# A modulation vector's work moved from a dense layer into the mixer before it, and that layer in two phases by seven products

## The reference, cut to what matters

```python
def rms_norm(x, g): ...
for layer in range(2):
    mod = silu(c) @ ada_w[layer] + ada_b[layer]        # 1024 -> 6 * 1024
    shift_m, scale_m, gate_m, shift_f, scale_f, gate_f = split(mod, 6)
    h = rms_norm(x, norm_mix_g[layer]) * (1 + scale_m) + shift_m
    x = x + gate_m * (hybrid mixer(h) if layer == 0 else conv module(h))
    h = rms_norm(x, norm_ffn_g[layer]) * (1 + scale_f) + shift_f
    x = x + gate_f * ((silu(h @ w_gate[layer]) * (h @ w_up[layer])) @ w_down[layer])
return rms_norm(x, final_norm_g)                       # x: 256 rows of 1024
```

## Time and profile before

| | us |
|---|---|
| median of the runs | 1461.85 (1460.13 to 1463.21) |
| the profiled execution | 1465.13 |
| its span, first to last instruction | 1463.4 |

### The profile page before, as it was taken

How to read it: one execution, slowest core, us unless ns; L and a number is a source line. 1 busy time by engine, 2 the same in 40 slices (tenths; PEclk the granted TensorE clock), 3 DMA queues, 4 the chain that set the end, 5 groups by cost and what they waited for, 6 DMA issues and landing times. The chain is left out here.

```text
span 1463.4 us, 18944 instructions
## 1 busy us (share of the span) xinstructions
PE 1376.3 (94%) x7517; PEld 1015.5 (69%) x7517; DVE 870.7 (60%) x1464; ACT 275.6 (19%) x602; POOL 265.6 (18%) x342
## 2 busy tenths in 40 slices
PE   5999999896776999999999999999999999999997
PEld 1877655653442788768888888777766878888843
DVE  2458775432232668753454685788783874777864
ACT  2222221000000311643345101000002113211101
POOL 5078010000000300553355402100020100000000
PEclk9999999998888999999999999999999999999999
DMA  9976887899999697866774455898854552555431
GB/s 350 310 263 226 285 329 298 348 417 415 416 418 385 191 305 261 306 194 162 159 180 133 160 162 176 327 333 322 297 210 150 155 156 73 163 168 172 170 129 47
DMA packets 176057, 355.58 MB, mean 243 GB/s; under 512 B 7289, under 2 KB 137041, under 8 KB 158561
## 3 DMA queue, kind: packets, MB, share of 16 engines
q1 hardware_dynamic: 166720, 313.64, 60.4%
q0 software_dynamic: 9248, 40.71, 9.5%
HBM read 352.58 MB, written 1.74 MB: 242 GB/s over the span
## 5 line engine op out<-in xcount | busy, mean ns | idle before, releaser
L1846 PE MATMUL PS<-HT,ring 128*128 128x256 f32 x1152 | 258.3, 382 | 0.1
L1846 PEld LDWEIGHTS PS<-HT,ring 128*128 128x128 f32 x1152 | 215.5, 190 | 36.0 <-issue 7.9
L1542 DVE TENSOR_TENSOR X<-X,PS 128x1024 f32<-128x1024 f32 x14 | 17.1, 1222 | 113.2 <-PE PS L1318 113.2
L1265 PE MATMUL PS<-ring_extra,slot_rows 128*32 128x256 f32 x576 | 56.3, 450 | 27.6 <-DMA ring_extra<-in_expert_w_gate 7.1
L2876 PE MATMUL PS<-HT,ring 128*128 128x256 f32 x352 | 76.8, 379 | 0.0
L2905 PE MATMUL PS<-ada_stage,half_sums 128*128 128x256 f32 x320 | 75.6, 379 | 0.0
L2905 PE MATMUL PS<-ring,half_sums 128*128 128x256 f32 x320 | 75.6, 379 | 0.0
L2876 PEld LDWEIGHTS PS<-HT,ring 128*128 128x128 f32 x352 | 66.7, 190 | 9.0
L2882 PE MATMUL PS<-ring,hid 128*128 128x512 f32 x160 | 71.8, 592 | 0.0
L2905 PE MATMUL PS<-ring,HT 128*128 128x256 f32 x304 | 68.8, 379 | 0.0
L2905 PEld LDWEIGHTS PS<-ring,half_sums 128*128 128x128 f32 x320 | 59.4, 190 | 11.2 <-issue 4.3
(11 more groups left out here) (736 smaller groups left out, 2465.4 us busy)
## 6 DMA issues: line engine op xcount, KB each, us to landing
ring<-in_hy_w_in SPq DMA_DIRECT2D x40, 1024.0 KB, 8.4
ring_extra<-in_w_ada SPq DMA_DIRECT2D x24, 1024.0 KB, 7.9
ada_stage<-in_ada_w POOLq DMA_DIRECT2D x24, 1024.0 KB, 7.3
ring<-in_ffn_w_gate SPq DMA_DIRECT2D x22, 1024.0 KB, 5.9
ring<-in_ffn_w_up SPq DMA_DIRECT2D x22, 1024.0 KB, 5.8
ring<-in_ffn_w_down SPq DMA_DIRECT2D x22, 1024.0 KB, 5.8
ring_extra<-in_expert_w_down SPq DMA_DIRECT2D x18, 1024.0 KB, 22.9
ring_extra<-in_expert_w_up SPq DMA_DIRECT2D x18, 1024.0 KB, 20.1
```

The lines of the kernel that those rows point to most:

```text
L1265: mm = pe.matmul(PS[e * SLOTS:(e + 1) * SLOTS, 2, j * CW:(j + 1) * CW], hs[:, k, e * SLOTS:(e + 1) * SLOTS], w[e][:, k, :], start=(k == 0) ...
L1542: dve.tensor_tensor(part, part, PS[:, 6:8, :], ALU.add).then_inc(added, 1)
L1846: mm = pe.matmul(dst, w[:, k, half * P:(half + 1) * P], HT[:, k, :], start=(k == 0), stop=(k == KT - 1))
```

## The change

- The third modulation's loads, adds, sums and transposes leave the first dense layer. In the mixer SP loads the 24 pieces in turns into two buffers (the memory of `BC`, and `stage`), DVE adds each at a position of `THIRD_ADDS` (one a quarter behind each attention slot from (23, 0) on), and PE sums the columns of finished vectors into bank 7 and transposes them at three positions; ACT copies in between and DVE finishes. The sums stay in a memory of their own, `third_acc`. The values of attention and one part of the out projection wait for bank 7.
- Four more small loads stand in POOL's list at the mixer's start, two fewer in the tail's.
- The first dense layer takes the form of the second, and its weights' order; DVE forms the sums of its first gate and up chunk at the mixer's end.
- The biases of layer 1's two gates are loaded as broadcast rows and added by DVE where the gate rows were copied; POOL builds the blocks of the convolution's taps after the first layer.

```diff
+    carry = ExitStack()
+    third_acc = sb(carry, "third_acc", [P, 5, D])
+    THIRD_AT = (2, 0, 3)
+    GATE_MIX, GATE_FFN = 0, 4
+    carried_sums = third_acc[:, 1:4].rearrange("p j (k n) -> p j k n", k=4)
...
+                    (third_bias[:, 0:2, :], t["ada_b"][1][0:2 * D].rearrange("(s p k) -> p s k", p=P, k=KT)),
+                    (third_bias[:, 2:4, :], t["ada_b"][1][3 * D:5 * D].rearrange("(s p k) -> p s k", p=P, k=KT)),
+                    (third_gains[:, 0, :], t["norm_mix_g"][1].rearrange("(p k) -> p k", k=KT)),
+                    (third_gains[:, 1, :], t["norm_ffn_g"][1].rearrange("(p k) -> p k", k=KT)),
                 ]
                 for dst, src in loads:
                     pool.dma_start(dst, src).then_inc(small, 16)
-        SMALLS = SMALLS_BEFORE + 16 * 16
+        SMALLS = SMALLS_BEFORE + 16 * 20
...
+        THIRD_ADDS = ((20, 2), (21, 1), (21, 2), (22, 0), (22, 2), (23, 1), (24, 0), (24, 3), (25, 2), (26, 1), (27, 0), (27, 3),
+                      (28, 2), (29, 1), (30, 0), (30, 3), (31, 2), (32, 1), (33, 0), (33, 3), (34, 2), (35, 1), (35, 3), (36, 2))
...
+        third_rows_at = {(25, 0): 0, (31, 0): 1, (36, 3): 2}
+        third_turn_at = {(25, 2): 0, (31, 2): 1, (37, 1): 2}
+        third_finish_at = {(25, 3): 0, (31, 3): 1, (37, 1): 2}
+        THIRD_PARTS = ((2, 3), (1,), (3,))
+        THIRD_READY = (8, 16, 24)
+        wv3 = t["ada_w"][1].rearrange("(p k) (g n) -> p k g n", k=KT, n=2 * D)
...
+                def fetch_third(a):
+                    if a == 0:
+                        sp.wait_ge(used, base + V0 + 3)
+                    elif a == 1:
+                        sp.wait_ge(cols, 1)
+                    else:
+                        sp.wait_ge(third_summed, a - 1)
+                    sp.dma_start(third_stage[a % 2].rearrange("p (a n) -> p a n", a=1), wv3[:, ds(a % KT, 1), a // KT, :])\
+                        .then_inc(third_in[a % 2], 16)
+
                 for s in range(NP + 12):
+                    for a in range(THIRD):
+                        if (THIRD_ADDS[a - 2] if a > 1 else ((19, 1), (20, 1))[a]) in ((s, 0), (s, 1)):
+                            fetch_third(a)
...
+                    for a in range(2, THIRD):
+                        if THIRD_ADDS[a - 2] in ((s, 2), (s, 3)):
+                            fetch_third(a)
...
+                    pe.wait_ge(third_made, 2 if m >= 4 else 1)
...
+                def sum_third(c):
+
+                    pe.wait_ge(third_summed, THIRD_READY[c])
+                    if c:
+                        pe.wait_ge(moved_att, 4 * c)
+                    for g in range(2 * len(THIRD_PARTS[c])):
+                        v = third_acc[:, THIRD_PARTS[c][g // 2], :].rearrange("p (m h k) -> p h k m", h=2, k=KT // 2)[:, g % 2]
+                        mm = pe.matmul(PS[32 * g:32 * g + 32, 7, :], ones[:, 0:32], v, start=True, stop=True,
+                                       tile_position=(0, 32 * g))
+                    mm.then_inc(third_rowsum, 1)
+
+                def turn_third(c):
+                    n = 64 * len(THIRD_PARTS[c])
+                    pe.wait_ge(third_rowcopy, c + 1)
+                    for k in range(KT // 2):
+                        mm = pe.transpose(PS[:, 7, k * P:k * P + n], third_rows[0:n, k * P:(k + 1) * P], ident[0:n, 0:n])
+                    mm.then_inc(third_cols, 1)
...
+                pe.wait_ge(third_made, 3)
                 out_half(0, 1)
...
+                        act.wait_ge(third_rowsum, c + 1)
+                        act.activation(third_rows[0:n, :], PS[0:n, 7, :], ACT.Copy).then_inc(third_rowcopy, 1)
...
+                def add_third(a):
+                    g, k = a // KT, a % KT
+                    dve.wait_ge(third_in[a % 2], 16 * (a // 2 + 1))
+                    dst = third_acc[:, THIRD_AT[g]:THIRD_AT[g] + 2, :].rearrange("p a n -> p (a n)")
+                    if k == 0:
+                        dve.tensor_scalar(dst, third_stage[a % 2], cv[:, 0:1], None, ALU.mult).then_inc(third_summed, 1)
+                    else:
+                        dve.wait_ge(third_summed, a)
+                        dve.scalar_tensor_tensor(out=dst, in0=third_stage[a % 2], scalar=cv[:, k:k + 1], in1=dst,
+                                                 op0=ALU.mult, op1=ALU.add).then_inc(third_summed, 1)
+
+                def finish_third(c):
+                    dve.wait_ge(third_cols, c + 1)
+                    columns = PS[:, 7, :].rearrange("p (k g x) -> p g k x", k=KT // 2, g=4)[:, :, :, 0]
+                    shift, scale = ((0, 1), (0, None), (None, 0))[c]
+                    home = (mod, mod_next, mod_next)[c]
+                    by_half = lambda ap: ap.rearrange("p (h k) -> p h k", h=2)
+                    if shift is not None:
+                        ins = dve.tensor_tensor(by_half(home[:, 0, :]), columns[:, 2 * shift:2 * shift + 2],
+                                                by_half(third_bias[:, (0, 2)[c], :]), ALU.add)
+                    if scale is not None:
+                        step(dve.tensor_tensor(by_half(mcol[:, 0, :]), columns[:, 2 * scale:2 * scale + 2],
+                                               by_half(third_bias[:, 1 if c == 0 else 3, :]), ALU.add))
+                        ins = dve.scalar_tensor_tensor(out=home[:, 1, :], in0=mcol[:, 0, :], scalar=1.0,
+                                                       in1=third_gains[:, 0 if c == 0 else 1, :], op0=ALU.add, op1=ALU.mult)
+                    ins.then_inc(third_made, 1)
...
+                first_gate, first_up = (segs["ffn0"].base + j for j in range(2))
+                for n in (first_gate, first_up):
+                    dve.wait_ge(landed[slots[n]], 16 * turns[n])
+                gate, up, (t1, t2, t4) = w_slot(first_gate), w_slot(first_up), (out_sum0[:, j] for j in range(3))
+                step(dve.tensor_tensor(t1, up[:, 0:4, :], gate[:, 0:4, :], ALU.subtract))
+                step(dve.tensor_tensor(t2, up[:, 4:8, :], t1, ALU.subtract))
+                step(dve.tensor_tensor(up[:, 0:4, :], up[:, 4:8, :], up[:, 0:4, :], ALU.subtract))
+                step(dve.tensor_tensor(t4, gate[:, 4:8, :], t2, ALU.subtract))
...
-            ffn(0, 0, turn_vectors, modulation_rows)
-            modulation_columns()
-            gate_rows(1, 0, 0)
-            pe.wait_ge(gated, 4)
-            turn(1)
+            for e in range(FFN_CHUNKS):
+                split_gate_up(0, e, 0)
+                if e == 0:
+                    turn_vectors()
+            for gi in range(len(DOWN_GROUPS)):
+                split_down(0, gi)
+            whole_down(0)
+            turn_row(1, 0)
+            gate_rows(GATE_MIX, 0)
+            turn_row(1, 1)
...
+            dve.wait_ge(small, SMALLS)
+            dve.tensor_tensor(gate_a[:], gate_a[:], PS[:, 0:2, :].rearrange("p a b -> p (a b)"), ALU.add).then_inc(moved, 1)
...
+            dve.wait_ge(biased, 16)
+            dve.tensor_tensor(gate_b[:], gate_b[:], PS[:, 0:2, :].rearrange("p a b -> p (a b)"), ALU.add).then_inc(moved, 1)
...
+            pool.wait_ge(x_done, 4)
+            pool.dma_start(gate_b[:], t["ada_b"][1][5 * D:6 * D].partition_broadcast(P)).then_inc(biased, 16)
...
```

More of the change, by code:

```diff
@@ L167, in segment @@
         stream.extend(sources)
-    def expert_order(n):
-        order = [("g", 0), ("u", 0)]
-        for e in range(1, n):
-            order += [("g", e), ("u", e), ("d", e - 1)]
-        return order + [("d", n - 1)]
     QUAD = 4
@@ L2929, in seven @@
                 hs7 = lambda j: [hsum[:, j, k, :] for k in range(4)]
-                ws7 = lambda j: [wsum[:, e % 2, j, k, :] for k in range(4)]
-                arrive(pe, n_g)
-                arrive(pe, n_u)
-                pe.wait_ge(combined, weights_summed(f, e))
-                if e > 1:
-                    pe.wait_ge(combined, row_sum(f, e - 1, 2))
-                product(P2, rows(1, 0), half(gate, 1))
-                product(P1, rows(0, 0), half(gate, 0)).then_inc(used, 1)
-                if e > 1:
-                    pe.wait_ge(combined, row_sum(f, e - 1, 5))
@@ L3007, in split_gate_up @@
-            def split_gate_up(e, norm):
-                n_g, n_u = chunk(1, "g", e), chunk(1, "u", e)
-                gate, up = w_slot(n_g), w_slot(n_u)
-                half = lambda ap, h: [ap[:, 4 * h + k, :] for k in range(4)]
-                rows = lambda h, i: [HT[:, 4 * h + k, i * P:(i + 1) * P] for k in range(4)]
-                hs7 = lambda j: [hsum[:, j, k, :] for k in range(4)]
-                ws7 = lambda j: [wsum[:, (e + 1) % 2, j, k, :] for k in range(4)]
+                ws7 = lambda j: [wsum[(e + 1) % 2][:, j, k, :] for k in range(4)]
@@ L3724, in _program @@
     tail.close()
+    carry.close()
 def _constants(np):
```

607 lines of the change are left out of this document (183 added, 424 removed).

## The result

The changed kernel takes **1490.56 us** (median; 1488.98 to 1501.66) against 1461.51 (1460.13 to 1463.21) beside it: a ratio of 1.0213, 95% interval 1.0175 to 1.0251, all of it above 1. The forecast was 1465.3 with a range up to 1473.0. So the change is slower, as forecast, but by 29 us and not by 3.4. The profiled execution took 1490.99, its span 1489.2.

The account below looks back on a forecast made before the run. PE, busy nearly throughout, was taken to bound the kernel. First layer −13.2, junction +1.9, moved PE work +5.2, waits for adds +7.9, mixer's start +0.8 and attention's start +0.8 gave +3.4: 1465.3 us against the median, range 1456.0 to 1473.

Parts of the forecast that it names:

- The first layer: First dense layer: in the second layer's form it takes 207.0 plus 0.5 instead of 220.7 us, a gain of 13.2.
- The first sum's wait: Mixer's attention: PE waits 2.5 to 3.8 us before the first column sum for DVE's add 7, +3.1.
- The values of pairs 0 and 4: Mixer's attention: PE waits before these values, 0.85 to 1.5 us (+1.1) and 0.55 to 1.3 (+0.9).
- the edits at nothing: Edits priced at zero: DVE's four sums, SyncE's new waits, ScalarE's copies, POOL's waits and DVE's wait for an add's loads.
- PE's own work: Column sums and transposes moved into the mixer: 1.95 + 0.98 + 0.98 + 3 × 0.44, a loss of 5.2 us.
- their loads 4.9 to land: Mixer: loads of the third modulation's adds take 4.9 us to land, 9.9 at most.
- The third rival: Mixer: DMA engines can't carry the added loads; +4 and up to +11 above the forecast, 1471; chance 20 in 100.
- The shares add up: DMA rival: biases, weights and third modulation share the engines, needing 15.4 to 17.8 us per 14.4 us period of two slots.
- Two stage buffers: DMA rival: two stage buffers and six weight chunks store some 7 of the 11 us excess over 5.5 periods.
- The place where it decides: DMA rival's sign: DVE idle before adds, released by stage loads, or PE waiting for ring chunks between 690 and 810.
- no part of the sum is clock: Whole sum: granted clock at its upper level, 1.00 in the attention chunks and 0.99 in the last stretch, so no clock term.
- may get in DVE's way; I take +1.9, between 1.4 and 4: Junction to the convolution: 6.9 us after the layer's end, +1.7; POOL's four tap blocks may disturb DVE, so +1.9.

Follow-up runs that it names:

- d1: c2 with each load of the third modulation cut to 128 of 2048 columns, all 24 adds kept: 1459.78 us, ratio 0.9985.
- d2: c2 with 16 of the third modulation's 24 pieces, whole loads, adds spaced wider, last third left out: 1463.2 us, ratio 1.001.
- e2: Changed kernel with each load of the third modulation cut to 128 of 2048 columns, adds kept: 1472.54 us, ratio 1.0064.
- e9: Changed kernel with the attention's bias loads issued from ACT's queue, not POOL's, same bytes: 1487.36 us, ratio 1.0167.
- e4: Changed kernel with the fifth add moved behind the last move of y_T, from (22, 2) to (23, 0): 1483.31 us, ratio 1.0146.
- e1: Changed kernel with POOL's four tap blocks held back until DVE has spread the gate: 1492.58 us, ratio 1.0187.
- e5: Changed kernel with the tap blocks built by DVE and POOL's output-bias work held until DVE's convolution chains are done: 1488.11 us, ratio 1.0183.
- c2: s1 with e5, adds 4 to 9 later, and the gate rows ahead of the first row's transposes: 1476.08 us, ratio 1.0086.
- s1: Changed kernel with two column sums of four groups in place of three, the first at (28, 0): 1489.51 us, ratio 1.0194.
- e3: Changed kernel with the second pair's bias loads issued after the first slot's scores have their bias: 1490.13 us, ratio 1.0188.

## Why the prediction was wrong

**Right, with their sizes.** The first layer: −13.1 for a forecast of −13.2. The mixer's start: 8.71 from the first product to the setup in both kernels, so the four small loads cost nothing here (+0.8 taken); in the profiles of d1 and d2 PE waits 0.5 and 0.8 for one of them (`third_gains`), which is the term's size. The first sum's wait 2.2 (+3.1 taken), the second's, with short loads, 1.24 (+2.1). The values of pairs 0 and 4 never waited (+1.1 and +0.9): no line of theirs stands among PE's waits. Of the edits at nothing, DVE's four sums cost nothing that shows: the first layer takes 207.6 with them ahead of it. So the forecast's count of DVE against PE, with loads left out, was too dear: 4.2 of waits in e2. That the whole mixer of e2, +14.0, comes so near the forecast's +14.7 is luck: fewer waits cancel against 7.1 of PE's own work for 5.2 and a rest of 2.6 that the forecast did not have.

**Wrong, the main step: "their loads 4.9 to land".** This price is from 480 to 640, and the step put it into a stretch where the DMA engines have other work. The trace of before held the better row: in 667 to 668, the very place of the late piece, a weight load of the same size took 17.1:

```profile
ring<-in_hy_w_in SPq DMA_DIRECT2D x1, 1024.0 KB, 17.1
```

The piece that came late took 18.5, the medians of the two buffers were 7.8 and 11.1, and the loads' bytes cost 20.3 us (e2). The third rival had the mechanism, PE's waits as the end of a chain from late pieces over DVE's queue, and was mis-sized: it gave +4 to +11 and a chance of 20 in 100. Its steps against the runs:

1. *The shares add up.* The queues in 640 to 830, before and after:

```profile
q1 hardware_dynamic: 22166, 22.36, 37.1%
q0 software_dynamic: 1936, 6.82, 23.9%
```

```profile
q1 hardware_dynamic: 21034, 42.30, 64.3%
q0 software_dynamic: 1921, 6.76, 21.7%
```

From 61 to 86%, and 86% of a stretch that its own waits made longer: 163 us of engine time, which is 96% of the 170 us that would be left without e2's 20.3 (an estimate from these numbers). Biases cost 6.1 us a MB over the whole (21.7% of 190 us for 6.76 MB), a little under the lower of the rival's two prices, and everything on the hardware queue 2.9: that makes 15.5 of 14.4 us a period, its lower sum. So the sum of the shares was not what failed, but that it took 7 us of the excess as stored by buffers. The rule of the Trainium skill that the prediction weighed ("DMA: Bandwidth & Descriptors", Issuing engines are not separate DMA queues) is borne out: the transfers of SP, POOL and, in e9, ACT share the engines, and changing the queue gave little.

2. *Two stage buffers.* A piece's load is issued once its buffer's add is done. With an add each 7.2 us a piece has two such periods less one add, 2 × 7.2 − 2.4 = 12.0, to land in. Of the 24 pieces in 640 to 830, 7 took longer, 12.7 to 18.5. And ahead of the attention the adds stand closer: the late piece could be issued only when the add at (21, 2) was done, 3.0 us before DVE came to its own add. There the buffers stored nothing. At 4.9 it would have been late for DVE by 1.9 and for PE not at all (an estimate; in e2 DVE waits 2.70 at this add, and PE doesn't wait).

3. *The place where it decides.* The prediction looked for DVE idle between 690 and 810 and took 0 to 3 for the attention's start. The add at (22, 2) stands ahead of the last `y_T` move, so the first late piece hit PE at 675, for 13.1, with a lowered clock behind it. e4 takes that step alone away: some 7 us.

Of the mixer's +34.3, PE's own work is 7.1, its waits are 22.4 (13.1 + 2.2 + 6.3 + 0.8), and 4.8 is left. Here the prediction's "no part of the sum is clock" failed: the score behind the first wait and its 24 products are 2.0 longer at the lowered clock. The rest is not laid to a cause here; e2 keeps 2.6 of such a rest without the long wait, and d1 3.2, of which 1.5 is the clock at the mixer's end.

**Wrong, the junction: "may get in DVE's way; I take +1.9, between 1.4 and 4".** It is +7.5. The order of gate rows and transposes cost +2.8 to +3.0 (the junctions of 8.0 and 8.2 in e1 and e5, where nothing disturbs DVE; c2, with the gate rows first, has 5.3), which the bound held. Of it +1.7 was in the sum, and the other 1.1 to 1.3 is again the clock: the gate rows take 3.15 (e1) and 3.32 (e5) in that place, and not 1.88. The tap blocks cost the other 4.5 to 4.7, for which the term held 0.2 and its upper bound 2.3. The edit had a cover named (the taps are wanted 55 us later), but the cover is for POOL; nothing hid it from DVE.

**Wrong by a little, PE's own work: +7.1 for +5.2.** Sums of two groups were priced at half of four. They take as long:

```profile
710.52 2.02 PE L2041 MATMUL PS<-third_acc,ones 128*32 128x512 f32 x8 [2.22 <-DVE third_acc L2475]
...
777.99 2.02 PE L2041 MATMUL PS<-third_acc,ones 128*32 128x512 f32 x4 [6.30 <-DVE third_acc L2475]
```

The Trainium skill has the rule that would have priced them ("TensorE: Matmul & The Clock Gate", Why this matters for your kernels: products with few output columns, each in its own group of 32 columns, run at the same time). Both rows agree with it. It also makes the two sums of s1 cheaper than the change's three.

## What to carry to other kernels

Price a moved load at the landing time of loads of its size in the stretch that it moves to, and add up the engines' booked time there before and after. Then compare, for each load, the time from its issue to the instruction that needs it: a mean share that fits says nothing of a load that has 3 us. Then ask what stands *behind* the waiting instruction on its engine: a late piece of something that nobody needs yet became PE's longest wait, through a 0.47 us instruction that happened to be queued after it. Moving the add that waited gave some 7 us back (e4), moving two of the transfers beside it nothing (e3), and in c2 a wait of the same length came back at another place. Last, a wait of PE can cost more than its length: what follows it ran at the lower clock here.

## What the runs showed of the hardware that was not expected

- A DVE instruction can be held by several POOL instructions in a row: 7.58 for 0.74 beside four that took 7.54 in all. The other direction shows in the attention: the first of these POOL adds takes 0.74, the second, beside a DVE add of 2.34, 2.85. That is POOL's side, for which the prediction had no row.

```profile
702.06 0.74 POOL L2745 TENSOR_TENSOR rows_q<-x_scores 128x256 f32<-128x256 f32 x1 [6.00 <-ACT x_scores L2275]
702.88 2.85 POOL L2746 TENSOR_TENSOR rows_q<-rows_q,x_scores 128x256 f32<-128x256 f32 x1
```

  The Trainium skill ("SBUF — State Buffer", Who interferes with whom) states that the two, where both need the port that they share, exclude each other for whole instructions, whoever is first. The rows agree in both directions, and go further: DVE wasn't let in between POOL's instructions.
- The same bias bytes cost 5.9 us of engine time a MB from POOL's queue and 4.9 from ACT's, both well above the 2.9 of weights and pieces (the hardware queue after: 64.3% of 190 us for 42.30 MB).
- The same four products on PE took 1.88 right behind the layer's products (c2) and 3.15 to 3.37 after PE had been idle for 2.56 (e1, e5, after), at granted clocks of 0.56 to 0.59.
- The first block, which no kernel here changes, ended anywhere in a span of 6 us from profile to profile, so that stages have to be compared from a start of their own.
